# Hybrid decoder block with a hierarchical mixture of experts: the first two expert blocks gathered before the last token tile is routed, the first block's products in plain fp32, the router on residual rows

## What is computed

```python
def hybrid_layer(h, ...):
    u = rms_norm(h, g_mix)
    proj = u @ w_in
...
    h = h + jnp.concatenate([attn, conv], axis=-1) @ w_out
    h = h + hierarchical_moe(rms_norm(h, g_ffn), w_rg, b_rg, w_re, b_re, w_gate, w_up, w_down)

def hierarchical_moe(u, w_rg, b_rg, w_re, b_re, w_gate, w_up, w_down):
    g_p, g_idx = lax.top_k(softmax(xt @ w_rg + b_rg), 1)
    e_p, e_idx = lax.top_k(softmax((xt @ w_re + b_re) of that group), 2)
    gates = g_p * e_p / jnp.sum(e_p, axis=-1, keepdims=True)
...
    def expert_block(args):          # xb: 128 rows of xt, e: their expert
        hdn = jax.nn.silu(xb @ w_gate[e]) * (xb @ w_up[e])
        return hdn @ w_down[e]
```

## Time and profile before

| | us |
|---|---|
| median of 3 runs | 1234.68 (1234.14 to 1235.44) |
| the profiled execution | 1235.03 |
| its span | 1233.3 |
| attention ends (last `times_v` product) | 604.3 |
| product G of tile 7 starts | 631.6 |
| gate product of block 0 done (`sil` starts) | 650.1 |
| rows of block 2 turned | 672.4 |
| TensorE busy | 1136.9 (92%) |
| VectorE / ScalarE / GpSimd busy | 643.3 / 539.6 / 227.4 |
| moved by DMA | 291.57 MB |

### The profile page before, as it was taken

How to read it: one execution, slowest core, us unless ns; L and a number is a source line. 1 busy time by engine, 2 the same in 40 slices (tenths; PEclk the granted TensorE clock), 3 DMA queues, 4 the chain that set the end, 5 groups by cost and what they waited for, 6 DMA issues and landing times.

```text
span 1233.3 us, 18330 instructions
## 1 busy us (share of the span) xinstructions
PE 1136.9 (92%) x6758; PEld 856.0 (69%) x6758; DVE 643.3 (52%) x929; ACT 539.6 (44%) x813; POOL 227.4 (18%) x261
## 2 busy tenths in 40 slices
PE   6999999999998999999878999988989898999977
PEld 5999988899995666766657776655556555555533
DVE  6423242334336566667489865445554544445547
ACT  7212241144335455545327755445544454444520
POOL 4000001130300111010142423222222221222110
PEclk9999999999999999999999999999999999999998
DMA  9420015424005233221569999999999999999995
GB/s 270 104 70 1 1 35 195 147 106 138 1 1 137 87 103 87 86 69 69 220 237 384 356 372 404 421 416 390 397 406 380 403 396 397 405 392 392 385 362 234
DMA packets 66061, 291.57 MB, mean 236 GB/s; under 512 B 10489, under 2 KB 36137, under 8 KB 53457
## 3 DMA queue, kind: packets, MB, share of 16 engines
q1 hardware_dynamic: 48176, 243.38, 52.1%
q0 software_dynamic: 16528, 42.66, 9.1%
q10 hardware_dynamic: 1296, 4.72, 0.9%
HBM read 269.57 MB, written 37.93 MB: 249 GB/s over the span
## 4 chain that ended last, share of the span: by engine, by line
PE 58%; DMA 21%; DVE 8%; ACT 6%; issue 6%; POOL 1%; DVEq 0%; SPq 0%; ACTq 0%; POOLq 0%
DMA wu<-in_w_up 18%; PE ps L1124 10%; PE ps L1126 10%; PE ps L1125 10%; PE ps L1494 4%; PE ps L1445 3%; PE ps L1447 3%; PE ps L1446 3%; PE ps L1252 2%; PE ps L1234 2%; PE ps L1220 2%; PE ps L1432 2%; ACT wu_high L1842 1%; DVE probs L2274 1%; ACT yb L1891 1%
## 5 line engine op out<-in xcount | busy, mean ns | idle before, releaser
L2326 DVE TENSOR_TENSOR wu_low<-wu,wu_high 128x2048 fp32r<-128x2048 f32 x36 | 81.1, 2287 | 57.7 <-ACT wu_high L1842 57.7
L1459 PE MATMUL ps<-wu,xa 128*64 128x512 f32 x224 | 102.1, 598 | 0.0
L1459 PE MATMUL ps<-wg,xa 128*64 128x512 f32 x224 | 102.1, 598 | 0.0
L1842 ACT ACTIVATE wd_high<-wd 128x2048 fp32r<-128x2048 f32 x36 | 66.8, 1905 | 79.6 <-DMA wd<-in_w_down 77.8
L2326 DVE TENSOR_TENSOR wd_low<-wd,wd_high 128x2048 fp32r<-128x2048 f32 x36 | 81.2, 2288 | 33.5 <-ACT wd_high L1842 33.3
L1842 ACT ACTIVATE wu_high<-wu 128x2048 fp32r<-128x2048 f32 x36 | 66.9, 1906 | 70.3 <-DMA wu<-in_w_up 70.3
L2326 DVE TENSOR_TENSOR wg_low<-wg,wg_high 128x2048 fp32r<-128x2048 f32 x36 | 81.1, 2288 | 19.3 <-ACT wg_high L1842 19.3
L2435 DVE TENSOR_TENSOR hid<-sil,ps 128x512 f32<-128x512 f32 x18 | 12.3, 686 | 131.7 <-PE ps L1447 131.7
L1842 ACT ACTIVATE wg_high<-wg 128x2048 fp32r<-128x2048 f32 x36 | 67.1, 1907 | 25.0 <-DMA wg<-in_w_gate 24.0
L1025 POOL DMA_INDIRECT expert_rows<-yb,idxs x30 | 45.7, 1522 | 156.4 <-ACT yb L1891 134.3
L1494 PE MATMUL ps<-wd,ha 128*64 128x512 f32 x224 | 54.3, 630 | 21.1 <-ACT ha L1885 21.1
(11 more groups left out here) (430 smaller groups left out, 3025.0 us busy)
## 6 DMA issues: line engine op xcount, KB each, us to landing
wg<-in_w_gate SPq DMA_DIRECT2D x32, 2048.0 KB, 16.6
wu<-in_w_up SPq DMA_DIRECT2D x32, 2048.0 KB
wd<-in_w_down SPq DMA_DIRECT2D x32, 2048.0 KB, 20.1
u_rows<-u POOLq DMA_DIRECT2D x16, 512.0 KB, 6.2
raw_c<-in_w_in SPq DMA_DIRECT2D x5, 1024.0 KB, 5.4
xin<-in_x SPq DMA_DIRECT2D x8, 512.0 KB, 11.6
zx<-in_x POOLq DMA_DIRECT2D x4, 1024.0 KB, 7.2
conv_part_rows<-zx POOLq DMA_DIRECT2D x16, 256.0 KB, 2.9
```

Of the source, the lines that this page charges most:

```text
L1459: last = mm(ps[HALF * n:HALF * (n + 1), 7, :], xa[:, k, :], raw[m][:, 1, k, :], start=(k == 0), stop=(k == KT - 1))
L1842: A(flat_half(wh[m][:, :, :], n), flat_half(raw_kf(m, s), n), ACT.Copy).then_inc(w_high[m], 1)
L2326: return V.tensor_tensor(flat_half(wl[m][:, s, :, :], n), flat_half(raw_kf(m, s), n), flat_half(wh[m][:, :, :], n).bitcast(F32), ALU.subtr ...
```

## The change

Six things are changed at once.

1. **Router on residual rows.** U0 and U1 turn `h1b` itself (into `h1T`) and no longer `u2`. The norm's gain is multiplied into the router weights once (`wr` by `gffnT`, near the start), and the row factor `ms` is applied to the logits in LT. Nothing on the way to the logits waits for U2 any more, so U2 moves behind LT for tiles 0 to 5 and behind L for tile 6, and URS one step later. In RT one instruction compares both experts.
2. **Tail of tile 7 in halves.** ACT squares the attention rows straight from PSUM; root, `aT`, `aTh`, `aTl` and W0, W1 go by halves of the columns.
3. **Gather early.** Job FIRST is run for tile 6 only. POOL gathers rows of tiles 0 to 6 for blocks 0 and 1 into cleared buffers (`first_x`, `xg`); rows of tile 7 have a number outside the bound and stay zero. When tile 7 is routed, its tokens are added by products of `h1g` (residual by gain) with a one-hot matrix that holds the row factor (`last_rows`), into the same PSUM as the turned gathered rows (`fixed_rows`).
4. **Block 0 in plain fp32.** `whole` multiplies `x_first` with the raw weights: 8 fp32 products in place of 24 for each of gate and up, no high and low parts of weights or tokens.
5. **Loads.** `first_load` of expert 1's up matrix no longer waits; its down matrix waits for tile 7's row factor.
6. **Order.** On DVE, job S of tile 7 and the five instructions that write `plan` now stand behind `placehot`, S behind everything of the plan. Fill products are fewer.

```diff
-PE_TAIL = [("M", R7), ("W0", R7), ("G", R6), ("W1", R7), ("FIRST", R6), ("U0", R7), ("U1", R7), ("L", R7),
-           ("LT", R7), ("G", R7), ("CNT", 0), ("FIRST", R7), ("KIND", 0)]
...
+PE_TAIL = [("M", R7), ("G", R6), ("W0", R7), ("FIRST", R6), ("W1", R7), ("U0", R7), ("U1", R7), ("L", R7), ("LT", R7)]
+STREAMED = {("G", R6): 2, ("W0", R7): 5, ("U1", R7): 1, ("L", R7): 2, ("LT", R7): 2}
...
             first_load("g", 1)
-            sp.wait_ge(xg_in[0], 16)
-            wait_x_made(sp, ("L", R7))
-            for m in "ud":
-                first_load(m, 1)
+            first_load("u", 1)
+            sp.wait_ge(u2rs_ready, NT)
+            first_load("d", 1)
...
+                    pool.wait_ge(rows_out, 32 * R7)
+                    pool.wait_ge(idx_ready, 2)
+                    gather_first(0, first_x[:, :])
...
+            fixed_rows(0, first_x)
+            stream(3, 6)
+            extra("G", R7)
+            last_rows(0, low_ks)
+            extra("CNT", 0)
+            last_rows(0, high_ks)
+            extra("KIND", 0)
+            whole("g", range(6))
             extra("PLACE", 0)
-            product("g", 0, 0, 0, high_ks)
-            turn_tokens(1, 1)
-            product("u", 0, 0, 0)
+            whole("g", range(6, KT))
+            fixed_rows(1, xg[:, 1, :])
+            last_rows(1, range(KT))
+            whole("u", range(KT))
...
+            def fixed_rows(s, src):
+
+                pe.wait_ge(xg_in[s], 16)
...
+                for k in range(KT):
+                    mm(big[:, P * k:P * (k + 1)], src[:, k::KT], ident[:, :], start=(k % 4 == 0), stop=False)
+
+            def last_rows(s, ks):
...
+                for k in ks:
+                    last = mm(big[:, P * k:P * (k + 1)], h1g[:, k::KT], rank_hot[:, s, :], start=False, stop=(k % 4 == 3))
...
+            def whole(m, ks):
...
+                    last = mm(ps[:, {"g": 2, "u": 3}[m], :], x_first[:, k, :], raw[m][:, 0, k, :],
+                              start=(k == 0), stop=(k == KT - 1))
```

More of the change, by code:

```diff
@@ L2337, in low_x @@
+            extra("U0", R7)
+            extra("U1", R7)
+            extra("L", R7)
+            extra("LT", R7)
+            extra("RT", R7)
+            places(R7)
+            hot(R7, 0)
+            extra("G", R7)
+            hot(R7, 1)
             def low_x(b, nth, s):
```

374 lines of the change are left out of this document (212 added, 162 removed).

## The result

| | before | after |
|---|---|---|
| median of 5 runs each, us | 1234.68 (1231.62 to 1236.32) | 1242.08 (1239.58 to 1243.01) |
| the profiled execution | 1235.03 | 1239.58 |
| its span | 1233.3 | 1237.9 |

A forecast was written before the change was run, and what follows sets the result against it. The hand-over after attention was taken as a chain of waits; attention 4.5 us less put G 6.8 earlier, the gate product 13.0, but late copy and table left 5.4: 1235.03 - 5.4 = 1229.6, by the median 1229.3; range 1222.5 to 1235.5.

The forecast's parts named there:

- Attention: Attention stage: TensorE's waits, mostly around U2 and the `pT` copies, shrink, ending it 4.5 us sooner (1 to 7).
- The index: Hand-over: row numbers for the first gather stand 10.9 us behind attention, from W0 and tile 6's work on VectorE.
- 19.0 us to `both`: Tile 7's router chain after attention: `both` ready after 19.0 us, 8 less than before, hidden behind the gather.
- The gather: Hand-over: the first gather takes 8.7 us under weight loads, landing 20.9 us behind attention.
- The identity and one-hot products: TensorE behind the gather: eight identity products take 1.15 us, four fp32 one-hot products 0.65.
- The clock: TensorE after waiting for the gather: identity and fill products partly at 1.2 GHz cost 1.5 us (0 to 2.6).
- The rival with a clock at half level through block 0: TensorE stays at 1.2 GHz from the gather wait through block 0: 2.7 us slower, 1237.4 us; chance 9%.
- What is late next: Before the expert loop: tile 7's late S delays copy and table, taking most of 13 us; 5.4 remain.
- the forecast's later way to the mark: Way to block 2's turning: table read of 9.7 us, then gather; rows at 667.0, against 666.4 through VectorE's entry.
- The mark as a measure of the end: Block 2's rows turned, 672.4 before: its shift, 5.4 us sooner, was taken as the change of the whole.
- returning waits: No-change rival: attention's waits return elsewhere (1 us gained, not 4.5), the copy takes 9.1; 0.9 less, 1234 us; chance 20%.
- the stream: Rival: the weight stream alone counts; removing about 10 us of DMA idle time gives 1224.7 us; chance 13%.

The follow-up runs named there:

- e2: The kernel before, with its read of `first_rows` issued at the end of attention, just behind the first weight load: 1233.76 us, 0.9993 of the kernel before.
- e8: The changed kernel without the last tile's 16 one-hot products in the first two blocks, transposes replacing identity products: 1241.25 us, 1.0045 of the kernel before.
- e13: e9 without the last tile's 16 one-hot products in the first two blocks, transposes replacing identity products: 1220.81 us, 0.9896 of the kernel before.
- e4: The changed kernel with job S of tile 7 moved back ahead of the plan on VectorE: 1236.0 us, 1.0005 of the kernel before.
- e3: The changed kernel with all first weight loads held until the read of `first_rows` has landed: 1227.63 us, 0.9941 of the kernel before.
- e9: The changed kernel with read and slots early, TensorE reordered behind the first gathered rows, loads held until the first gather landed: 1220.54 us, 0.9900 of the kernel before.
- e14: The same kernel as e9, measured again over more rounds: 1221.46 us, 0.9883 of the kernel before.

## Why the prediction was wrong, step by step

| mark | forecast | measured |
|---|---|---|
| attention ends | 599.8 | 593.5 |
| index behind it | +10.9 | +21.7 |
| gather issued | +12.2 | +23.1 |
| its time | 8.7 | 11.3 |
| G of tile 7 behind it | +25.0 | +39.8 |
| G to gate product done | 12.3 | 14.4 |
| G to VectorE's entry | 22.9 | 25.6 |
| entry to block 2 turned | 18.7 | 18.7 |

- **Attention: right in sign, too small.** 10.8 us in the profiled run and 9.8 by the mean of the fourteen profiles that share this code (ends 592.1 to 596.5, mean 594.5), against a range of 1 to 7; the code before ended at 604.3 and, in `e2`, at 603.5. TensorE's waits for `u` and for the `pT` copies are gone, and fewer came back than I had set aside. All its waits in attention were 16.9 us and are 8.0 now; the other 2 us are less busy time (202.3 to 200.3), which no run explains. The longest groups now (us in total, times, longest us):

```profile
PE ps L1126 <- DVE rk L2279: 2.0, 4, 0.8
PE ps L1284 <- DVEq L2223: 1.7, 3, 0.8
PE ps L1126 <- DVE aTl L2206: 1.3, 1, 1.3
PE ps L1254 <- DVE ot L2197: 1.3, 1, 1.3
PE ps L1301 <- DVE lgt L2243: 1.1, 1, 1.1
```

- **The index: the step that failed.** "the row numbers stand 10.9 us behind attention" was a count of VectorE's and TensorE's work alone. It held where the read was early (+10.4 in eight runs) or the loads alone were held (+10.9 in two), and was 10.8 short in the changed kernel. The kernel's read of `first_rows` had no place in my sum. It had landed by the end of attention in the trace I read, so I priced it at nothing, and did not look at where the change puts its issue: behind the two row copies, because U2 of tile 6 had moved behind LT. I had named those very copies as "issued 8 us later than now, against the weight loads", with 9.1 us each. They took 12.2 and 17.6, and what stood behind them in the queue was not followed. So contention with the loads was priced for the gather, and not for the copies and the read ahead of it. The "19.0 us to `both`" failed with the same read: it was 31.1, since VectorE's part of the router's chain stands behind `first_rows`. The prediction cited a rule for the gather, that transfers issued by SP, ACT and POOL interleave on the same 16 DMA engines (the Trainium skill, "Trainium Kernel Development and Optimization", Key Constraints), and the runs agree with it: the gather takes 4.4 us without loads and 11.3 with loads beside it.
- **The gather: a mis-sized term.** 11.3 us where I took 8.7 from the earlier trace rows. Those gathers ran beside one or two loads, this one beside a queue of five. With none it took 4.4 to 4.5, near the 4.7 of the earlier trace rows.
- **The identity and one-hot products: mis-sized.** 4.14 us for 1.15 and 2 x 2.17 for 2 x 0.65. I had priced a plain fp32 product of 128x128 like a transpose of that shape. The trace counts 16 instructions for the eight products and 8 for the eight transposes, and the earlier trace rows had the sign: the single product on `asq` stands there as x2. From the landed gather to G that made 5.4 us for 4.1, in which 1.5 was for the clock, and it is most of the 2.1 between G and the gate product. `e8` and `e13` show no cost of it at the end; `e8` is blurred by its clock.
- **The clock.** 1.5 us were set aside for identity and fill products at half clock. The granted clock was 0.50 (1.2 GHz) in 615 to 620 and 625 to 630, behind TensorE's idle 9.0 and 5.8 us, and the fill products ran at full clock (1.68); the identity products took 4.14 us, against 3.84 in block 1 at a granted clock of 1.00. The rival with a clock at half level through block 0 did not occur: its products ran at the granted clock of 1.00 from 635 on.
- **What is late next: right.** The second copy behind the late slots releases VectorE (10.7 us of idle, forecast "5 us or more"), the table follows behind, and `e4` priced it at 6 to 7 us. The copy took 8.3 against 7.5. But the forecast's later way to the mark, by the table and block 2's gather, was not the later one: the table read took 2.3 us for 9.7, and the rows landed at 671.1, 6 us before they were turned.
- **The mark as a measure of the end: right, but coarse.** From the turning of block 2 to the end of the span it was 560.9 us before and 560.4 after. Over the experiments it was 557.0 to 563.8, so it tells the end to 3 us or so and no better.
- **The sum.** At G the index is 10.8 us late, the gather 2.6 and its products 1.3, less 6.3 for attention: 8.5 behind the forecast's 624.8. VectorE's entry is 11.1 behind, the mark 10.5 and the profiled end 10.0 (1239.58 against 1229.6); the median lies 2.5 above that profile.
- **The rivals.** The slower side ended where I had put 9%, but by another mechanism. I had counted chances for returning waits, for the stream and for the clock, and none for a transfer that the change newly puts on the path.

## What to carry to other kernels

When a change moves the place from which a transfer is issued, redo the list of that queue from the order: every transfer behind it is late with it, also one that cost nothing before because it had landed in time. Small transfers that release a chain (an index, a gather, a table) should be issued, and if need be allowed to land, before a train of bulk loads starts; here holding the loads by 6.4 us against the end of attention gained 14 (`e3`). And test two suspected losses together before adding them, since here 0.0118 and 0.0054 gave 0.0110.

## What I had not expected of the hardware

A read of 1 KB took 2.7 to 2.8 us ahead of two 512 KB copies on its queue, 5.4 to 5.7 behind them, 6.9 beside weight loads without copies ahead, and 17.4 to 18.3 behind copies that themselves ran beside loads. The copies took 5.0 to 6.0 us without loads and 12.2 and 17.6 beside them. A gather of 128 rows of 4 KB took 4.4 us alone and 11.3 beside the train of loads; the second gather, which has row copies ahead of it on its queue as well, took 12.8 to 26.1.

The end of attention lay at 592.1 to 593.8 in some profiled runs and at 595.9 to 596.5 in others, of kernels with the same code up to there, two runs of one and the same kernel among them. The difference is made in one place. TensorE idles about 1 us near 530 in all of them, and the granted clock from 530 to 540 is 1.00 in those that end first, 0.83 in two (the changed kernel among them), and 0.66 in all that end late. The stretches 520 to 540 of `e9`, of the changed kernel, and of `e14`, which is `e9` once more:

```profile
520.00:530.00 10.00, 8.86 (x90) 6.86 (x91) 7.58 (x15) 7.82 (x17) 0.00 (x0) 1.00 0.01 2
530.00:540.00 10.00, 9.94 (x86) 7.49 (x86) 7.53 (x24) 4.05 (x10) 1.09 (x2) 1.00 0.66 197
...
520.00:530.00 10.00, 8.86 (x92) 6.86 (x90) 7.59 (x15) 7.70 (x18) 0.00 (x0) 1.00 0.01 2
530.00:540.00 10.00, 9.94 (x73) 6.96 (x72) 5.86 (x22) 2.86 (x6) 1.09 (x2) 0.83 0.64 197
...
520.00:530.00 10.00, 9.84 (x104) 7.50 (x102) 7.58 (x14) 7.84 (x17) 0.00 (x0) 1.00 0.07 28
530.00:540.00 10.00, 8.96 (x48) 6.82 (x50) 5.16 (x22) 1.97 (x4) 1.09 (x2) 0.66 0.62 185
```

The late ones reach this place up to 1 us later already and leave it 3 us later still. A single profile of this kernel cannot tell differences of 3 us at its end; medians, and distances behind a mark, tell more.
